# A recurrent stage on TensorE: score matmuls cut into 64x64 tiles, and the first corner round placed in front of the first score group

## The reference, cut to what matters

```python
def _wkv_scan(r, w, kh, ak, v, kt, reverse):
    def step(S, inp):
        r_t, w_t, kh_t, ak_t, v_t, kt_t = inp
        sk = jnp.einsum('bhvk,bhk->bhv', S, kh_t)
        S = S * w_t[:, :, None, :] - sk[..., None] * ak_t[:, :, None, :] + v_t[..., None] * kt_t[:, :, None, :]
        return S, jnp.einsum('bhvk,bhk->bhv', S, r_t)
    S0 = jnp.zeros((B, H, N, N), jnp.float32)
    _, o = lax.scan(step, S0, (r, w, kh, ak, v, kt), reverse=reverse)
    return o
```

## Time and profile before

| what | value |
|---|---|
| time, median of 3 runs | 3314.43 us (3310.67 to 3314.73) |
| span of the profiled execution | 3300.3 us |
| what the median of the runs has above that span | 14.1 us |
| PE busy | 3197.5 us, 97% of the span |
| weight loads busy | 2034.3 us, 62% |
| DVE busy | 1787.4 us, 54% |
| ACT busy | 1039.2 us, 31% |
| recurrence, first score matmul to last | 1418.4 to 1830.5 us: 412.1 us |
| in it: PE busy, DVE busy, ACT busy | 384.0, 250.6, 165.9 us |
| in it: PE records, weight load records | 12384, 12384 |
| packets of the instruction queue, whole span | 207, with 3.39 MB |

### The profile page before, as it was taken

The page is one execution under the profiler, slowest core; times in us unless marked ns, Lnnn a source line. Parts: engine busy times, 40 slices in busy tenths (PEclk is TensorE's granted clock), DMA queues, the critical chain, the costliest instruction groups (busy, mean ns, idle before and its releaser), DMA issues. The chain is left out here.

```text
span 3300.3 us, 59856 instructions
## 1 busy us (share of the span) xinstructions
PE 3197.5 (97%) x25976; PEld 2034.3 (62%) x25976; DVE 1787.4 (54%) x2945; ACT 1039.2 (31%) x1588; POOL 142.8 (4%) x94
## 2 busy tenths in 40 slices
PE   9999999999999899989999999999999999999997
PEld 4564565555555555577887555567666666666665
DVE  2337762677777479146666332245645446545446
ACT  2336652334333223333433452003321111221111
POOL 0000000000000000000000000024200000200002
PEclk9999999999999999999999999999999999999998
DMA  3221101334543523365655223211112112122211
GB/s 140 58 71 36 46 23 60 118 122 139 167 155 121 193 74 139 122 186 168 177 167 147 89 76 149 91 51 64 58 64 81 61 64 83 58 93 74 70 64 64
DMA packets 218822, 328.53 MB, mean 100 GB/s; under 512 B 55488, under 2 KB 176704, under 8 KB 213440
## 3 DMA queue, kind: packets, MB, share of 16 engines
q1 hardware_dynamic: 218560, 324.69, 30.1%
HBM read 221.74 MB, written 96.34 MB: 96 GB/s over the span
## 5 line engine op out<-in xcount | busy, mean ns | idle before, releaser
L655 PE MATMUL ra_ps<-xT,ring 128*128 128x512 f32 (+1 forms) x1152 | 429.8, 526 | 0.0
L1891 PE MATMUL tl_ps<-merged,pool 128*128 128x320 f32 x1440 | 405.1, 434 | 2.5 <-PEq L108 1.8
L1891 PEld LDWEIGHTS tl_ps<-merged,pool 128*128 128x128 f32 x1440 | 273.6, 190 | 118.4 <-issue 4.0
L655 PEld LDWEIGHTS ra_ps<-xT,ring 128*128 128x128 f32 x1152 | 214.3, 190 | 199.0 <-issue 189.3
L2155 DVE TENSOR_TENSOR oR<-tl_ps,oR 128x320 f32<-128x320 f32 x416 | 202.1, 489 | 151.7 <-PE tl_ps L1891 148.9
L1106 PE MATMUL rg_ps<-xT,ring 128*128 128x512 f32 (+1 forms) x720 | 264.9, 523 | 3.3 <-PEq L108 3.3
L1976 ACT ACTIVATE ring<-tl_ps 128x320 f32<-128x320 f32 x96 | 42.0, 437 | 533.7 <-PE tl_ps L1891 533.7
L1106 PEld LDWEIGHTS rg_ps<-xT,ring 128*128 128x128 f32 x720 | 134.5, 191 | 113.9 <-issue 108.4
L1891 PE MATMUL tl_ps<-hold,pool 128*128 128x320 f32 x720 | 202.6, 432 | 0.0
L2161 DVE TENSOR_TENSOR merged<-tl_ps,ring 128x320 f32<-128x320 f32 x96 | 47.2, 491 | 255.5 <-PE tl_ps L1891 140.0
L1891 PE MATMUL tl_ps<-xT,pool 128*128 128x320 f32 x640 | 182.7, 432 | 0.0
(11 more groups left out here) (254 smaller groups left out, 4718.3 us busy)
## 6 DMA issues: line engine op xcount, KB each, us to landing
pool<-ub SPq DMA_DIRECT2D x320, 160.0 KB, 2.8
ub<-ra_ub SPq DMA_DIRECT2D x32, 1280.0 KB, 5.4
pool<-in_w_ff SPq DMA_DIRECT2D x32, 1024.0 KB, 4.8
pool<-in_w_ff SPq DMA_DIRECT2D x64, 512.0 KB, 3.4
ring<-in_w_in SPq DMA_DIRECT2D x38, 512.0 KB, 3.7
ub<-ra_v SPq DMA_DIRECT2D x16, 640.0 KB, 6.8
mg_gate<-gates SPq DMA_DIRECT2D x16, 640.0 KB, 3.9
xT<-in_xT SPq DMA_DIRECT2D x15, 640.0 KB, 8.6
```

The costliest lines, as they stand in the source:

```text
L655: last = pe.matmul(ps[:, bank + j, 0:n], w[c][:, 128 * i:128 * i + 128], xT[:, i, t0:t0 + n], start=(i == 0), stop=(i == KT - 1))
L1891: last = pe.matmul(bank(n, b), lhs(k), rhs(k), start=(fresh and k == 0), stop=(k == d - 1), skip_group_check=True)
```

## The change

`scores` is written with 64x64 tiles: each of its matmuls becomes two, one for each half (m) of the 128 stationary columns, with the same moving operand. A group that had 4 matmuls now has 8, and the results lie where they did. And in every step the call `scores(g + 1, 0)`, which stood ahead of the first corner round, now stands behind it. Nothing changes on DVE, ACT, POOL and SP, nor in what any instruction waits for.

```diff
                 for j in range(2):
-                    for h in range(2):
-                        rows = slice(64 * h, 64 * h + 64)
-                        last = pe.matmul(ps[:, 4 + 2 * (q % 2) + h, 192 * j:192 * j + 192], x[rows, 2 * q + j, CH:3 * CH],
-                                         x[rows, 2 * q + j, 3 * CH:6 * CH], start=True, stop=True)
+                    for m in range(2):
+                        for h in range(2):
+                            last = pe.matmul(ps[half(m), 4 + 2 * (q % 2) + h, 192 * j:192 * j + 192],
+                                             x[half(h), 2 * q + j, CH + CH * m:2 * CH + CH * m],
+                                             x[half(h), 2 * q + j, 3 * CH:6 * CH], start=True, stop=True)
                 last.then_inc(sc_ready, 1)
...
             for g in range(NSTEP):
                 x, sc, v = ub[g % 3], SC[g % 2], X[g % 2]
-                if g + 1 < NSTEP:
-                    scores(g + 1, 0)
                 pe.wait_ge(masked, 4 * g + 4)
...
                 last.then_inc(x_ready, 1)
                 if g + 1 < NSTEP:
+                    scores(g + 1, 0)
                     if g:
                         pe.wait_ge(u_done, 2 * g)
```

## The result

The changed kernel takes 3343.1 us (median of 4 runs, 3337.0 to 3344.7) against 3312.6 us for the kernel before: a ratio of 1.009, with a 95% interval of 1.0075 to 1.0105. It is 30.6 us slower. The forecast was 3355 us, slower, with 3328 to 3376 as its range.

What follows compares the result with a forecast made beforehand. The prediction took instruction fetch to bound the recurrent stage: span 3300.3 plus 41.5 us for added packets is 3341.8, plus 14.1 for runs over span is 3355.9, less 1 for slack boundaries: 3355 us, range 3328 to 3376.

Steps and rivals of the forecast that it cites:

- What bounds: Recurrent stage: runs at the pace of its own instruction fetch, about 253 instructions per 4.10 us; chance 0.80.
- Rival A: Recurrent stage: fetch is hidden, stalls stay at 27 us and PE's saving arrives; 3290 us, or 3277; chance 0.07.
- The array's terms: Score groups on PE: 64x64 tiles cost 0 in streaming; fewer shape changes save 0.61 us a step.
- rival C: Score groups: four 64x64 tiles do not stream together at 192 columns; some 80 us slower, 3395; chance 0.04.
- The gain from fewer changes of shape: PE's steps: ten tile-shape changes become five; 0.93 us a step, 0.61 after waits on DVE, 24 us in 40 steps.
- The added fetch: Recurrent stage: 2560 added instructions make 10.1 packets at 4.10 us each, 41.5 us; bounds +30 to +63.
- rival B: Recurrent stage: fetch bounds but speeds up when asked earlier, a packet every 3.7 us; time stays at 3313; chance 0.06.
- The base of the sum: Whole kernel: profiled span of 3300.3 us, plus the 14.1 us by which the runs' median exceeds the span.
- Issue waits: PE in the recurrent stage: waits for its next instruction rise from 27 us to about 92.
- Rival D: PE in the recurrent stage: clock falls to 1.2 GHz in the longer stalls; 10 to 20 us more; chance 0.03.

Runs made afterwards that it cites:

- the thinned pair: The kernel before and the changed kernel, both with many short matmuls left out (values, line 1380, most of both corner rounds): 3248.4 and 3237.6 us.
- before_less: The kernel before without 7 of 8 of the values matmuls of line 1319, zeros in their place: 3288.7 us, ratio 0.9929.
- before_thin: The kernel before without 7 of 8 values matmuls, all of line 1380 and 12 of 16 matmuls in each corner round: 3248.4 us, ratio 0.9811.
- the swap alone: The kernel before with only the first score group moved behind the first corner round, tiles still 64x128: 3309.8 us against 3313.0, ratio 0.9997.
- corners_twice: The kernel before with the first corner round written twice in each step, 2560 more instructions: 3342.0 us against 3311.4, ratio 1.0098.

## Why the prediction was right

- **What bounds.** Right. The stage is held up by its instruction fetch, and the time goes with the instruction count in five kernels (+2560: +31 to +33 us, three times; -2184: -24 us; +376: -1 us, no change). Rival A, a hidden fetch, is out.
- **The array's terms.** Four 64x64 tiles do stream together at 192 columns, so rival C is out: a stream takes 323 ns as before, and a group at the full clock without a stall 0.88 us at most. The prediction said 0.8. The gain from fewer changes of shape is real but was sized too high: 0.61 us a step against (3248.4 - 3237.6) / 40 = 0.27 in the thinned pair. The wait for ACT's `Bs` behind group 2 took 8.5 us of it. With a full second corner round that wait may be shorter. This mistake hardly reached the time, since most of PE's gain became issue waits.
- **The added fetch: the term that was mis-sized.** 10 packets were added, as worked out. The sum gave them 41.5 us, at the stage's mean of 4.10 us each; by the medians they cost 30.6 us, 3.0 each, which is near the low end of the prediction's own bounds (+30). This is the 12 us by which 3355 is too high. The likely reason is in the prediction, as what it held for rival B and set aside: "a boundary without a stall may have asked for its packet late, so 4.10 may hold some of PE's own pace". Against it stood that no stretch in the earlier trace rows is shorter than 4.01 us, but those are distances from stall to stall. From the start of one packet to the next the trace of before has 3.40 to 5.10 us, and 19 of 95 distances are under 3.8: for one, a packet starts at 1566.50 and the next at 1569.90. The sentence "the pace is the same whether a stretch shows much idle time or little" does not hold either: before_less has its packets 4.34 us apart (92 of them in 395.2 us), and before_thin, where PE has no issue wait, 5.34. A mean distance is PE's pace where PE is the slower and the fetch's where that is. That one packet more costs less than this mean because 63 of 98 boundaries had no stall to begin with is my reading; no run shows the price of a single packet. Rival B's time, no change, was wrong all the same.
- **The base of the sum, and a piece of luck.** In spans the sum looks exact: 3341.8 was forecast, and it was 3341.1. That is luck. The 14.1 us by which the runs' median exceeded the span of before are no time ahead of the first and behind the last instruction: in the runs whose time and span are both known that is 1.8 us (3342.9 against 3341.1; 3306.5 against 3304.7 for the swap alone). The profiled execution of before comes to about 3302 by this, and none of its timed runs lies below 3305.5: it was some 10 us faster than a usual one. A base 10 us too low and a fetch term 11 us too high cancelled in the span. Taking the 14.1 us along did put the base of the runs right. By an estimate the stage before usually takes nearer to 420 us than 412: 3312.6 less 1.8, less the 2889 to 2895 us that lie outside the stage in the traces of the changed kernel, the swap alone and before_less.
- **Issue waits** rose to 72 us, not 92. The stage lengthened by 39.7 us in the trace, about as forecast, so the 20 us missing are mostly what was not saved on PE: its busy time fell by 9.8 us, and not by 24. Part of that is work at half clock, as follows.
- **Rival D**, the clock, happened, eight times in the stage's trace (once behind the wait of 3.6 us at its start and seven times with issue stalls of 1.6 to 2.4 us), but not with the 10 to 20 us that it had. I had given it 0.03 because the mean clock of the stage before reads 1.00 although it has a wait of 3.6 us. That was a misreading: a mean over 412 us hides 3 us. A short window of PE in the kernel before, right behind that wait, has 0.51:

```profile
1418.40:1421.40 3.00, 2.86 (x16) 0.51 0.81 234
```

  In this stretch of the changed kernel PE stands still for 2.24 us, and the clock falls to the lower level (1.2 GHz), where a score group takes 1.56 us instead of 0.88. Windows of PE first (the number behind the parenthesis is the clock):

```profile
1515.00:1517.10 2.10, 0.00 (x0) 0.96 0.52 161
1517.10:1520.50 3.40, 3.39 (x77) 0.52 0.21 57
1520.50:1523.50 3.00, 2.86 (x91) 1.00 0.66 193
```

and the timeline there:

```profile
1517.11 0.37 PE L1380 MATMUL rc_ps<-pool,rc_S 64*64 64x64 f32 x2 [2.24 <-issue]
...
1518.11 1.56 PE L1312 MATMUL rc_ps<-pool 64*64 64x192 f32 x16
```

  What the falls cost can be bounded from the same trace: from 1430 to 1860 us, 13 of the 102 distances from packet to packet overlap a stretch at half clock, and they are 4.50 us in the mean, against 4.11 for the other 89. That is some 5 us in all, and not all of it need be the clock's, since each fall comes with a long stall. That the rest costs nothing because the next packet is still on its way is my reading, argued and not shown.

## What to carry to other kernels

Count the instructions of a dense stretch before cutting a matmul into smaller tiles, and compare their rate with what the instruction queue delivers: here some 253 in 4.15 us in the mean and 3.4 us at the least. Stalls called "issue" that stand at equal distances in instructions, not in time, are the sign of it. Where they were, 31 us less work on PE brought nothing (the changed kernel against corners_twice), and each matmul of 32-bit floats cost four instructions. Take the price of a packet from a run that changes only the count: the mean distance between packets overstated it, 4.1 us against 3.0.

## What the runs showed that I had not expected

With 18 MB instead of some 64 MB moved in the stage the kernel gained 19 us, though a fetch, from the packet's start to PE's resumption, took 2.5 us in both; through what the gain came is open. And TensorE's clock fell to its lower level with single instruction stalls, one of 2.24 us, in a stage where PE is busy 374 of 452 us.
